# Quarters of the output projection: evictions ahead of the copies in the sample's steps, the first quarter's sums inside these steps, later sums and spreads sooner

## What is computed

```python
x = x + mixed @ p['w_out']
x = x + memory_attend(x, mem_k, mem_v, p['g_mem_q'], p['w_mem_q'], p['w_mem_o'])
y, conv_new = conv_ffn(x, conv0, p['g_ffn'], p['w_ffn_up'], p['w_ffn_conv'], p['b_ffn_conv'], p['w_ffn_down'])
x = x + y

def memory_attend(x, mem_k, mem_v, g, w_q, w_o):
    q = (rmsnorm(x, g) @ w_q).reshape(B, T, MEM_HEADS, MEM_HD)
    s = jnp.einsum('bqhd,bkhd->bhqk', q, mem_k) * MEM_SCALE
    o = jnp.einsum('bhqk,bkhd->bqhd', softmax(s), mem_v).reshape(B, T, MEM_HEADS * MEM_HD)
    return o @ w_o

def conv_ffn(x, conv_prev, g, w_up, w_conv, b_conv, w_down):
    u = rmsnorm(x, g) @ w_up
    ...
def rmsnorm(x, g):
    return x * rsqrt(mean(x * x, axis=-1) + EPS) * g
```

## Time and profile before

| | before |
|---|---|
| median of 3 runs | 1678.94 us |
| profiled execution, its own time | 1679.68 us |
| its span | 1677.9 us |
| TensorE busy | 1626.7 us (97%) |
| VectorE busy | 1172.2 us (70%) |
| ScalarE busy | 673.1 us (40%) |
| GpSimd busy | 466.2 us (28%) |

### The profile page before, as it was taken

One profiled execution on the slowest core, in us unless ns is written; L12 is line 12 of the kernel. 1 busy time (PEld: TensorE's weight loads), 2 busy tenths in 40 slices (PEclk: granted clock), 3 DMA queues, 4 the chain that ended last, 5 costly groups with the idle time before them and its releaser, 6 DMA issues.

```text
span 1677.9 us, 29423 instructions
## 1 busy us (share of the span) xinstructions
PE 1626.7 (97%) x11153; PEld 1501.1 (89%) x11153; DVE 1172.2 (70%) x1612; ACT 673.1 (40%) x1283; POOL 466.2 (28%) x244
## 2 busy tenths in 40 slices
PE   9999999999999999999887999999999999999998
PEld 8999889776667799998777999999999999999987
DVE  7583587896656655447397888878787867766765
ACT  7320222586566541215244455555555542011022
POOL 2583142000000224423025333322233322333432
PEclk9999999999999999999998999999999999999999
DMA  5322210330212324326211222221212226223213
GB/s 210 104 76 82 74 57 29 111 96 5 100 64 72 112 80 139 109 95 278 76 64 51 79 78 78 78 78 64 74 58 78 78 100 243 74 87 106 84 58 113
DMA packets 73125, 154.88 MB, mean 92 GB/s; under 512 B 29777, under 2 KB 37169, under 8 KB 70225
## 3 DMA queue, kind: packets, MB, share of 16 engines
q1 hardware_dynamic: 70736, 144.28, 25.3%
q10 hardware_dynamic: 2304, 9.44, 1.6%
HBM read 118.56 MB, written 32.86 MB: 90 GB/s over the span
## 4 chain that ended last, share of the span: by engine, by line
PE 86%; DVE 7%; issue 3%; ACT 2%; POOL 1%; DMA 0%; SPq 0%; DVEq 0%; ACTq 0%; POOLq 0%
PE scores L2740 20%; PE scores L3467 19%; PE bank L2740 10%; PE bank L3467 8%; PE pair L2740 7%; PE scores L3046 3%; PE bank L3106 3%; PE pair L3130 2%; PE scores L2836 2%; PE scores L2758 1%; DVE kbuf L2235 1%; PE pair L2749 1%; PE scores L3069 1%; PE pair L3164 1%; PE pair L3160 1%
## 5 line engine op out<-in xcount | busy, mean ns | idle before, releaser
L3467 PE MATMUL scores<-c,up_w 128*128 128x288 f32 x2464 | 363.1, 297 | 4.4 <-ACT kept_a L1789 3.2
L3467 PEld LDWEIGHTS scores<-c,up_w 128*128 128x128 f32 x2464 | 342.6, 189 | 5.7 <-issue 2.8
L1167 POOL TENSOR_TENSOR w_hi<-w_raw,zero 128x1024 fp32r<-128x1024 f32 x30 | 59.3, 1975 | 530.9 <-DVE prob L2251 262.2
L2740 PE MATMUL scores<-s_hi,w_down 128*128 128x384 f32 (+2 forms) x484 | 132.9, 334 | 0.0
L1908 ACT ACTIVATE s_hi<-s_raw 128x1152 fp32r<-128x1152 f32 x22 | 24.3, 1158 | 178.6 <-DMA s_raw<-s_mid 178.6
L2740 PEld LDWEIGHTS scores<-s_hi,w_down 128*128 128x128 f32 x484 | 88.1, 188 | 0.6
L1301 POOL TENSOR_TENSOR w_down<-down_raw,zero 128x1024 fp32r<-128x1024 f32 x20 | 37.9, 1894 | 175.4 <-PE scores L2740 80.2
L3467 PE MATMUL bank<-c,up_w 128*128 128x288 f32 x528 | 79.6, 301 | 5.2 <-DVE ext L2568 5.2
L2740 PE MATMUL scores<-act_hi,w_hi 128*128 128x384 f32 x240 | 81.7, 340 | 0.9 <-POOL w_lo L1170 0.9
L2667 DVE TENSOR_TENSOR xd<-scores,xd 128x384 f32<-128x384 f32 x108 | 58.8, 553 | 33.3 <-PE scores L2740 33.3
L1170 POOL TENSOR_TENSOR w_lo<-w_raw,w_hi 128x1024 fp32r<-128x1024 f32 x30 | 81.2, 2708 | 2.4
(11 more groups left out here) (475 smaller groups left out, 4261.9 us busy)
## 6 DMA issues: line engine op xcount, KB each, us to landing
w_raw<-wstream SPq DMA_DIRECT2D x40, 512.0 KB, 3.6
s_raw<-s_mid SPq DMA_DIRECT2D x11, 1152.0 KB, 5.3
up_raw<-wstream SPq DMA_DIRECT2D x22, 512.0 KB, 4.2
x<-wstream SPq DMA_DIRECT2D x22, 512.0 KB, 4.4
s_mid<-conv SPq DMA_DIRECT2D x22, 512.0 KB, 2.8
down_raw<-wstream SPq DMA_DIRECT2D x22, 512.0 KB, 5.1
x_blk<-xT ACTq DMA_DIRECT2D x8, 576.0 KB, 4.5
x_mid<-x_blk ACTq DMA_DIRECT2D x8, 576.0 KB, 3.1
```

The costliest lines, as they stand in the source:

```text
L1167: pool.tensor_tensor(w_hi[:, k], w_raw[:, k], zero[:].unsqueeze(2).to_broadcast([P, KB, P]), ALU.add).then_inc(w_rounded, 1)
L2740: mm = pe.matmul(out, w[:, k, at + kb], x(kb), start=first and kb == 0 and n == 0, stop=last and kb == n_kb - 1 and n == 2)
L3467: mm = pe.matmul(bank[acc][:, 0:QF], up_w[i][:, w, tile(kb)], b[:, kb], start=i in (0, 1, 3) and kb == 0 and n == 0, stop=kb == 3 and n == ...
```

## The change

On VectorE, in steps 9 to 14, the eviction is moved from the end of the step to ahead of the copy of the transposes. On ScalarE the square of an evicted part is made in the same step, first after the exponentials, and not one step later at the end. Quarter 0's additions are made in steps 10 to 12, its sums are issued behind product 4, its root in step 13, its reciprocal at the head of VectorE's step 14, and its spread behind product 5. For that, quarter 0 uses banks 0 and 2 (`SUM_BANKS`, `SPREAD_BANKS`), quarter 2 bank 6, and quarters 1 and 3 bank 7; the banks of products 6 to 15 are dealt out anew, and product 9 waits for the scaling of quarter 0, which reads bank 2. The sums and spreads of quarters 1 and 2 are issued one product sooner, the spread of quarter 3 one hidden product sooner. The lists of VectorE and ScalarE after the steps are reordered: scaling and rounding of each quarter come sooner between the evictions, and after the last one `join(0, 1, 0)` comes ahead of the parts of the second pair.

```diff
@@ -161,10 +161,11 @@
 MO_EARLY = 6
 MO_TILES = (3, 5, 7, N_MEM)
 MO_LAST = range(N_MO - 4, N_MO)
-MO_BANKS = [(1, 3)] * MO_EARLY + [((0, 1), (2, 3), (4, 5))[(d + 2) % 3] for d in range(N_MO - MO_EARLY)]
-
-
-SUM_BEHIND, SPREAD_BEHIND = {6: 0, 9: 1, 13: 2}, {7: 0, 10: 1, 14: 2}
+MO_BANKS = [(1, 3)] * MO_EARLY + [(4, 5), (0, 1), (4, 5), (2, 3), (0, 1), (4, 5), (2, 3), (0, 1), (2, 3), (4, 5)]
+
+
+SUM_BEHIND, SPREAD_BEHIND = {4: 0, 8: 1, 12: 2}, {5: 0, 9: 1, 13: 2}
+SUM_BANKS, SPREAD_BANKS = (0, 7, 6, 7), (2, 7, 6, 7)
 
 
 def mo_counted(d):
@@ -1718,6 +1719,11 @@
                     act.wait_ge(x_summed, summed_no(q - 1, 4 - j))
                 act.activation(quarter_square(q, j)[:], mo_part(4 * q + j), ACT.Square).then_inc(x_squared, 1)
 
+            def quarter_roots(q):
+                act.wait_ge(sum_ready, Q_FFN + q + 1)
+                act.activation(quarter_root[0:NF, q], bank[SUM_BANKS[q]][0:NF, 480:483], ACT.Sqrt, bias=eps[0:NF],
+                               scale=1.0 / D).then_inc(sum_used, 1)
+
             def round_output(c):
                 act.wait_ge(*((m_pv, c + 1) if c < NTILE else (m_turned, c - NTILE + 1)))
                 act.activation(om_part(om_hi, c), om_source(c), ACT.Copy).then_inc(om_rounded, 1)
@@ -1734,6 +1740,8 @@
                                               qm[:, :, TP:T].rearrange("p h (q b t) -> p b q h t", b=2, t=DS)[:, bb],
                                               ACT.Copy)
                     last.then_inc(qm_pair_ready, 1)
+                if n > NTILE:
+                    square_quarter(*divmod(n - NTILE - 1, 4))
                 if n - 3 >= NTILE:
                     round_output(n - 3)
                 if NTILE <= n - 2 < N_MEM:
@@ -1748,13 +1756,8 @@
                     memory_scale(n)
                 if 0 <= n - 2 < NTILE:
                     round_output(n - 2)
-                if n > NTILE + 1:
-                    square_quarter(*divmod(n - NTILE - 2, 4))
-
-            def quarter_roots(q):
-                act.wait_ge(sum_ready, Q_FFN + q + 1)
-                act.activation(quarter_root[0:NF, q], bank[6 + q % 2][0:NF, 480:483], ACT.Sqrt, bias=eps[0:NF],
-                               scale=1.0 / D).then_inc(sum_used, 1)
+                if n == N_MEM + 1:
+                    quarter_roots(0)
 
             def round_part(p, i):
 
@@ -1819,27 +1822,25 @@
                 act.wait_ge(conv_done, 2 * u + 2)
                 act.activation(conv[:, 0, 0:EXT - 2], conv[:, 0, 0:EXT - 2], ACT.Silu).then_inc(silu_done, 1)
 
-            square_quarter(1, 1)
             square_quarter(1, 2)
-            quarter_roots(0)
+            round_part(0, 0)
             act.wait_ge(w_split, W_END)
             round_up(0, 0, 0, 0)
             round_up(0, 0, 0, 1)
             square_quarter(1, 3)
-            round_part(0, 0)
+            round_part(0, 1)
             round_up(0, 0, 0, 2)
             square_quarter(2, 0)
-            round_part(0, 1)
+            quarter_roots(1)
             square_quarter(2, 1)
-            quarter_roots(1)
             round_up(0, 0, 0, 6)
             square_quarter(2, 2)
+            round_part(0, 4)
             square_quarter(2, 3)
-            round_part(0, 4)
             round_part(0, 2)
             square_quarter(3, 0)
+            quarter_roots(2)
             square_quarter(3, 1)
-            quarter_roots(2)
             round_part(0, 5)
             round_part(0, 3)
             square_quarter(3, 2)
@@ -2451,7 +2452,7 @@
                 dve.wait_ge(x_out[q % 2], 64 * (q // 2) + 64)
                 for m in range(4 * half, 4 * half + 4):
                     last = dve.scalar_tensor_tensor(x[:, m, quarter(q)], x[:, m, quarter(q)], const("g_ffn", m),
-                                                    bank[6 + q % 2][:, 0:QF], ALU.mult, ALU.mult)
+                                                    bank[SPREAD_BANKS[q]][:, 0:QF], ALU.mult, ALU.mult)
                 last.then_inc(b_made, 1)
 
             def combine(p, n):
@@ -2480,6 +2481,10 @@
                     memory_query(GH - 1, NCH - 1)
                 if 0 <= n - 3 < NTILE:
                     split_output(n - 3)
+                if n == N_MEM + 2:
+                    quarter_inverse(0)
+                if 0 < n - NTILE <= MO_EARLY:
+                    memory_residual(n - NTILE - 1)
                 if 1 <= n <= N_MEM:
                     c = n - 1
                     dve.wait_ge(mt_done, 2 * c + 2)
@@ -2503,55 +2508,54 @@
                                           ALU.mult).then_inc(m_norm, 1)
                 if n - 3 >= NTILE:
                     split_output(n - 3)
-                if n - NTILE >= 4:
-                    add_square(0, n - NTILE - 3)
+                if 2 <= n - NTILE <= 4:
+                    add_square(0, n - NTILE - 1)
+                if n - NTILE == 4:
+                    add_rows(0)
                 if n - NTILE == 6:
-                    add_rows(0)
-                if 0 < n - NTILE <= MO_EARLY:
-                    memory_residual(n - NTILE - 1)
-
-
-            add_square(1, 1)
+                    add_square(1, 1)
+
+
+            scale_rows(0, 0)
             memory_residual(6)
+            scale_rows(0, 1)
             add_square(1, 2)
-            quarter_inverse(0)
             memory_residual(7)
-            scale_rows(0, 0)
             add_square(1, 3)
             add_rows(1)
+            split_part(0, 0)
             memory_residual(8)
-            scale_rows(0, 1)
-            split_part(0, 0)
+            split_part(0, 1)
+            quarter_inverse(1)
             memory_residual(9)
-            split_part(0, 1)
             add_square(2, 1)
-            quarter_inverse(1)
+            scale_rows(1, 0)
             memory_residual(10)
             add_square(2, 2)
-            scale_rows(1, 0)
             scale_rows(1, 1)
+            combine(0, 0)
             memory_residual(11)
-            combine(0, 0)
             combine(0, 1)
-            memory_residual(12)
             add_square(2, 3)
             add_rows(2)
             combine(0, 2)
+            memory_residual(12)
             split_part(0, 4)
+            quarter_inverse(2)
+            split_part(0, 2)
             memory_residual(13)
-            split_part(0, 2)
             add_square(3, 1)
             combine(0, 3)
-            quarter_inverse(2)
+            scale_rows(2, 0)
             memory_residual(14)
             add_square(3, 2)
             split_part(0, 3)
-            scale_rows(2, 0)
+            scale_rows(2, 1)
             memory_residual(15)
-            scale_rows(2, 1)
+            split_part(0, 5)
             add_square(3, 3)
             add_rows(3)
-            split_part(0, 5)
+            split_part(0, 6)
 
             def fill_carried(u, ab):
                 if not (isinstance(u, int) and u == 0):
@@ -2594,16 +2598,15 @@
             dve.wait_ge(conv_moved, 16)
             for ab in range(2):
                 fill_carried(0, ab)
-            split_part(0, 6)
             quarter_inverse(3)
             join(0, 0, 0, True)
-            split_part(1, 0)
-            split_part(1, 1)
             scale_rows(3, 0)
             scale_rows(3, 1)
+            join(0, 1, 0, True)
+            split_part(1, 0)
             combine(1, 0)
+            split_part(1, 1)
             combine(1, 1)
-            join(0, 1, 0, True)
             combine(1, 2)
             join(0, 2, 0, True)
             split_part(1, 2)
@@ -3371,23 +3374,30 @@
             def quarter_sums(q):
 
                 pe.wait_ge(x_summed, summed_no(q, 4))
-                if q >= 2:
-                    pe.wait_ge(b_made, made_no("scaled", q - 2, 1))
+                if q == 1:
+                    pe.wait_ge(om_split, N_MEM)
+                if q == 3:
+                    pe.wait_ge(b_made, made_no("scaled", 1, 1))
                 for t in range(3):
-                    mm = pe.matmul(bank[6 + q % 2][0:NF, 480 + t:481 + t], stat[q % 2][:, 0, NF * t:NF * t + NF],
+                    mm = pe.matmul(bank[SUM_BANKS[q]][0:NF, 480 + t:481 + t], stat[q % 2][:, 0, NF * t:NF * t + NF],
                                    ones[:, 0:1], start=True, stop=True)
                 mm.then_inc(sum_ready, 1)
 
             def quarter_spread(q):
 
                 pe.wait_ge(rstd_ready, 3 + q)
-                if q == 1:
-                    pe.wait_ge(om_split, N_MEM)
                 for t in range(3):
-                    mm = pe.matmul(bank[6 + q % 2][:, NF * t:NF * t + NF],
+                    mm = pe.matmul(bank[SPREAD_BANKS[q]][:, NF * t:NF * t + NF],
                                    quarter_root[0:NF, q, t:t + 1].to_broadcast([NF, P]), ident[0:NF, 0:NF], start=True,
                                    stop=True)
                 mm.then_inc(y_spread, 1)
+
+            def sums_behind(d):
+
+                if d in SUM_BEHIND:
+                    quarter_sums(SUM_BEHIND[d])
+                if d in SPREAD_BEHIND:
```

(11 more changed lines are left out.)

## The result

| | kernel before | changed kernel |
|---|---|---|
| runs | 4 | 4 |
| median | 1678.55 us | 1669.49 us |
| lowest to highest | 1677.68 to 1679.61 us | 1668.23 to 1670.24 us |
| profiled execution, its span | 1677.9 us | 1667.5 us |
| ratio after / before, 95% interval | | 0.9945 [0.9928, 0.9962] |

The kernel before has one run more here than ahead of the prediction. The change saves 9.1 us by the medians, 10.4 us between the two profiled spans. 1667.5 us was forecast.

The account below looks back on a forecast made before the run. Bound: TensorE's eviction waits in the sample steps, then VectorE's work until 903.75 us. That stretch ending 12.4 us sooner, less 1 for the clock, saves 11.4: 1679.68 to 1668.3, or 1667.5 us against the median (chance 0.67); range 1663 to 1674.

Parts of the forecast that it names:

- The five waits, 7.6 us: Sample steps: TensorE's waits before five output-projection products for the previous product's eviction all go, -7.6 us.
- The product clock, 3.1 us: Sample steps: without 2 us gaps, two products at half clock (4.90 and 4.96 us) return to 3.40 us, -3.1 us.
- Product 5 ends near 821: End of the sample steps: product 5 ends 7.6 + 3.1 - 0.5 = 10.2 us sooner, near 821.
- The reserve of 0.5 us for the sums: Sample steps: 0.5 us taken off the gain before product 5's end, for quarter 0's sums issued behind product 4.
- VectorE's stretch, 70.4 us: From product 5's eviction to the last split: 62.9 work + 5.5 idle + 2 collisions = 70.4 us, 820.9 to 891.3.
- The choice of +2 between the bounds of -6 and +11.9: VectorE's stretch: GpSimd collisions add 2 us; -6.0 if all vanish, +11.9 if all 17.9 us of GpSimd are paid.
- Rival (b): VectorE's stretch: GpSimd's instructions collide nearly all, +8 us beyond the +2, giving 1676.3 us; chance 0.12.
- VectorE's idle time, forecast 5.5 us: VectorE's stretch: 3.8 us in five waits for ScalarE's square, plus 1.7 for last sample values' turn and last spread.
- within TensorE's slack both are free: Behind products 8 and 12: waits of some 2 us ahead of sums 1 and 2 cost nothing, given TensorE's 13 us slack.
- Rival (c): Second stretch: half clock becomes the bound, products cost 6.5 us instead of 3.25; 1682 us if 8 to 15 run so; chance 0.04.
- The 1 us put aside for the clock behind the last sums: After a gap of 3.5 us or more before the last sums the clock may fall: 1 us loss, between 0 and 1.5.
- Its own signs: Right: no eviction waits, products 3.4 us, first hidden product 10 to 13 us sooner. Wrong: half clock, stretch over 74 us.

Follow-up runs that it names:

- the first experiment: Changed kernel with VectorE's evictions in the sample steps back behind copy and split, ScalarE's square last in its step: 1676.65 us, ratio 0.9990.
- The seventh experiment: Changed kernel with ScalarE's rounding of the first three weight blocks ahead of its square of product 6: 1668.5 us, ratio 0.9944.
- the control: The changed kernel timed once more, with no further edit, in the third group of runs: 1667.82 us, ratio 0.9946.
- the version that took 5.8 us more off: Changed kernel with first three weight blocks rounded sooner, four VectorE reorderings, 4 and 18 unread matmuls ahead of sums 2 and 3: 1661.98 us, ratio 0.9905.

## Why the prediction was right, point by point, and what it mis-sized

**The five waits, 7.6 us: right.** None is left, and undoing this order alone returns 7 us.

**The product clock, 3.1 us: right in the profile, weaker as a cause.** All products in the steps take 3.2 to 3.4 us. But with the waits back, the first experiment kept full clock in the steps too. That the gaps cost the 3.1 us in the trace before is not shown; it happened in that execution.

**Product 5 ends near 821: 820.15.** The reserve of 0.5 us for the sums was about right (0.43 us at 815.19), and the spread of quarter 0 follows product 5 without a wait. The copies cost nothing behind the evictions: TensorE has no idle time from 795 to 820.15. The eviction came at 820.41, forecast 820.9.

**VectorE's stretch, 70.4 us: measured 74.5.** Its parts: work with collisions, forecast 62.9 + 2 = 64.9, measured 64.4. The choice of +2 between the bounds of -6 and +11.9 was about right: the collisions moved from scale_rows to the additions and splits (as the three rows beside GpSimd's above) and were not paid for every GpSimd instruction. Rival (b) did not come. The Trainium skill, "SBUF — State Buffer", section "Who interferes with whom", says that a VectorE instruction with two SBUF inputs contends with a GpSimd instruction that reads SBUF. The seventh experiment agrees: with GpSimd's work moved beside scale_rows, the addition took 0.76 us instead of 1.75.

**The mis-sized term: VectorE's idle time, forecast 5.5 us, measured 10.1 (74.48 - 64.39).** The five waits of 0.75 us for ScalarE's square came as forecast, 3.8 us. The 1.7 us for the last sample values and the last spread became 0.9 and 1.5 us. Not forecast: 2.5 us for product 13, 0.9 us for product 9, 0.4 us for ScalarE's part ahead of the join (881.27). The step that failed is this sentence of the prediction: "within TensorE's slack both are free", of the waits ahead of sums 1 and 2. They are free as time in which TensorE does nothing. But both were followed by half clock in this trace, and each time VectorE's next instruction was the eviction of the product that ran so. With the wait ahead of sums 2 filled, product 13 has full clock and the 2.5 us are gone. Rival (c) named this mechanism, but priced it only as a bound on all eight products, against the whole of TensorE's slack; one or two slow products are enough where the engine that sets the end needs just these. Its price of 6.5 us for a product at half clock was too high: product 13 took 5.6.

The 1 us put aside for the clock behind the last sums came too, but inside this stretch: TensorE waited 4.31 us ahead of sums 3, the clock was 0.50 from 873 to 877 us, and VectorE waited 1.5 us for the spread of quarter 3 (877.42). With unread matmuls ahead of sums 3 that wait was 0.7 us.

**The tail, 1 us of loss: a gain of 1.5 us, not forecast.** From the end of the last split on VectorE to the pair product it is 15.1 us (894.89 to 910.02), 16.7 before (903.75 to 920.43). TensorE waits 2.5 us at the second part's splits, as forecast. The gain is clock: behind the last split TensorE ran at 0.50 before and at 1.00 after (a window of each, before, then after; columns as in the earlier trace rows):

```profile
905.00:907.00 2.00, 2.00 (x10) 2.00 (x9) 2.00 (x2) 0.00 (x0) 2.00 (x1) 0.50 0.00 0
```

```profile
895.00:897.00 2.00, 2.00 (x15) 2.00 (x16) 2.00 (x1) 0.00 (x0) 2.00 (x2) 1.00 0.03 8
```

This comes and goes. All three kernels with the old order of the tail took 16.7 us here; of the ten traces with the new order, six took 15.1 to 15.2 us and four 16.55 to 16.83, with the half clock again. So the new order may help the clock, but the traces don't show that it holds it.

So the forecast of 11.4 us for the profiled execution came out as 10.4: start of the stretch 0.5 better, the stretch 4.1 worse, the tail 2.5 better, and roundings. That the total came so close is in part luck: the tail, where a loss was forecast, made up for more than half of what the stretch had lost.

**Its own signs.** Those of being right came with one exception: no wait of products 1 to 5, the spread without a wait, the loop behind unchanged, but the first hidden product only 8.2 us sooner (872.46 to 864.27), where 10 to 13 were named. One sign of being wrong came: VectorE's stretch took 74.5 us, over the 74 named. The other three did not: no half clock before 831 us, one addition of 1.75 us beside GpSimd where there were two before in this stretch (1.58 and 1.82 us), and full clock in the products of the quarters but for 9 and 13.

**The rest of the change: right to cost it at little.** The sums and spreads moved sooner, the new banks, the splits and the join together are worth 1.3 us between the medians (sample steps alone against the whole change, each against its own runs of the kernel before; 1.8 us against the control), with overlapping intervals, and the profiled stage does not show even that. Which of them would bring it stays open. The tail is a candidate: its 1.5 us of clock are as large.

## What to carry to other kernels

In a list that an engine works off in order, put the instruction that releases another engine's buffer ahead of those whose result is not awaited yet: here that was 7.8 of 9.1 us. A wait moved to an engine with slack costs nothing only if the engine's clock and the output that the bounding engine needs next are unharmed; read what stands right behind it. Where a vector engine bounds a stretch, count its idle time by releaser: here that pointed to the version that took 5.8 us more off.

## What the runs showed of the hardware

Waits of nearly the same length were followed by different granted clocks. Ahead of sums 2, after 2.31 us in the changed kernel and 2.32 us with the evictions behind the copies, product 13 ran at 0.50, in the changed kernel for 5.6 us; after 2.31 us in the control it ran so for part of its time; after 2.26 us with the old tail and 2.30 us with the weights sooner it ran at 1.00, 3.3 us. Nor is the shorter wait the safer one: after 1.34 us, in the kernel with VectorE reordered, product 13 ran at 0.50 from 852 to 854 us. Five waits of up to 1.9 us in the sample steps left the clock full, where five of up to 2.1 us in the trace before stood ahead of two products at half clock. What decides between them the runs do not show.

In the four traces with unread matmuls ahead of sums 2 the wait was 0.28 to 0.83 us, and product 13 ran at 1.00 in all four. Of the six traces with the sums at the same place and no such matmuls, two had that. That speaks for the matmuls as the cause, without leaving chance out.
